# Two operand buffers of a two-block transformer kernel, laid out with a start that steps by 64 bytes every four chunks

## What is computed

```python
    z = rmsnorm(h, norm2_w) @ mlp_w1
    h = h + jnp.square(jax.nn.relu(z)) @ mlp_w2
    ...
    proj = x @ w_in                                  # 2048 columns in, about 9.5 thousand out
    merged = g_a * (o_a @ w_o_dsa) + g_b * (o_b @ w_o_moba)
    return merged @ w_out
    ...
    g, u = jnp.split(x @ w_in, 2, axis=-1)
    return (jax.nn.silu(g) * u) @ w_out
```

## The kernel before

| operand | role | residue before |
|---|---|---|
| `x_even` (the residual's normed rows, in `xa`) | moving: wide mlp up and feed-forward in, and three-matmul projections of the second block; stationary: `mv` | 144 |
| `x_held` (in `xa`) | stationary: the second block's output projection | 240 |
| `xh` (mlp's inner rows, in the region) | stationary: mlp down | 240 |
| `xk` (memory rows) | moving in the first 30 us | 240 |
| `xa` with 272 or 258 columns | moving: high part 144, low part 0 | 144 and 0 |
| `xa` from column 16 on (`from_tokens`) | moving: high part 208, low part 64 | 208 and 64 |
| `xd` with 258 columns | moving: high part 224, low part 0 | 224 and 0 |

## Time and profile before

### The profile page before, as it was taken

How to read it: one execution, slowest core, us unless ns; L and a number is a source line. 1 busy time by engine, 2 the same in 40 slices (tenths; PEclk the granted TensorE clock), 3 DMA queues, 4 the chain that set the end, 5 groups by cost and what they waited for, 6 DMA issues and landing times.

```text
span 2573.8 us, 41371 instructions
## 1 busy us (share of the span) xinstructions
PE 2555.9 (99%) x15948; PEld 2297.6 (89%) x15948; DVE 1572.9 (61%) x2178; ACT 1189.7 (46%) x1609; POOL 27.9 (1%) x70
## 2 busy tenths in 40 slices
PE   9999999999999999999999999999999999999998
PEld 7999988888888888899999999988999888888886
DVE  5444856556556555565565566666876776656665
ACT  5543545434444344544444454444544445445442
POOL 1000000000000000000000000000000000000000
PEclk9999999999999999999999999999999999999999
DMA  7664556666555665574455565565576577567753
GB/s 251 179 180 130 165 181 180 196 196 186 190 184 191 196 195 186 173 224 154 131 165 170 160 200 183 186 213 161 150 205 180 189 196 191 189 186 186 195 196 114
DMA packets 467782, 468.80 MB, mean 182 GB/s; under 512 B 9246, under 2 KB 384142, under 8 KB 466862
## 3 DMA queue, kind: packets, MB, share of 16 engines
q1 hardware_dynamic: 465600, 459.31, 58.5%
q0 software_dynamic: 2064, 7.82, 0.9%
HBM read 464.93 MB, written 2.10 MB: 181 GB/s over the span
## 4 chain that ended last, share of the span: by engine, by line
PE 97%; DVE 1%; ACT 1%; DMA 0%; issue 0%; SPq 0%; DVEq 0%; ACTq 0%
PE ps L693 17%; PE ps L696 11%; PE ps L697 11%; PE ps L698 11%; PE ps L725 11%; PE ps L727 11%; PE ps L726 11%; PE ps L694 9%; PE ps L789 1%; DMA region<-in_mem 0%; PE ps L1130 0%; PE ps L1101 0%; DVE w_lo L2091 0%; PE ps L1137 0%; PE ps L1173 0%; PE ps L1006 0%
## 5 line engine op out<-in xcount | busy, mean ns | idle before, releaser
L2091 DVE TENSOR_TENSOR w_lo<-raw,w_hi 128x1024 fp32r<-128x1024 f32 (+1 forms) x867 | 1047.5, 1219 | 766.0 <-ACT w_hi L1438 764.5
L1438 ACT ACTIVATE w_hi<-raw 128x1024 fp32r<-128x1024 f32 (+1 forms) x869 | 902.1, 1051 | 909.4 <-PE ps L727 410.1
L693 PE MATMUL ps<-xa,w_hi 128*128 128x512 f32 x1920 | 666.0, 391 | 0.0
L696 PE MATMUL ps<-xa,w_hi 128*128 128x256 f32 (+2 forms) x2112 | 607.4, 288 | 0.0
L698 PE MATMUL ps<-xa,w_lo 128*128 128x256 f32 (+2 forms) x2112 | 595.0, 282 | 0.0
L697 PE MATMUL ps<-xa,w_hi 128*128 128x256 f32 (+2 forms) x2112 | 593.4, 281 | 0.0
L694 PE MATMUL ps<-xa,w_lo 128*128 128x256 f32 x1920 | 537.3, 280 | 0.0
L693 PEld LDWEIGHTS ps<-xa,w_hi 128*128 128x128 f32 x1920 | 360.1, 188 | 79.6
L697 PEld LDWEIGHTS ps<-xa,w_hi 128*128 128x128 f32 x2112 | 398.4, 189 | 2.0 <-issue 1.0
L696 PEld LDWEIGHTS ps<-xa,w_hi 128*128 128x128 f32 x2112 | 397.2, 188 | 3.2 <-issue 2.0
L698 PEld LDWEIGHTS ps<-xa,w_lo 128*128 128x128 f32 x2112 | 396.5, 188 | 0.0
(11 more groups left out here) (364 smaller groups left out, 2537.0 us busy)
## 6 DMA issues: line engine op xcount, KB each, us to landing
raw<-in_mlp_w SPq DMA_DIRECT2D x128, 1024.0 KB
raw<-in_w_in SPq DMA_DIRECT2D x106, 1024.0 KB
raw<-in_w_ffn_in SPq DMA_DIRECT2D x176, 512.0 KB
raw<-in_w_ffn_out SPq DMA_DIRECT2D x44, 1024.0 KB
raw<-in_w_out SPq DMA_DIRECT2D x32, 1024.0 KB
raw<-in_w_o_dsa SPq DMA_DIRECT2D x8, 1024.0 KB
raw<-in_w_o_moba SPq DMA_DIRECT2D x8, 1024.0 KB
raw<-in_w_kv_mem SPq DMA_DIRECT2D x7, 1024.0 KB
```

The costliest lines, as they stand in the source:

```text
L693: nc.tensor.matmul(o, hi, x.rearrange("p a n -> p (a n)"), start=opens and ci == 0, stop=False)
L696: nc.tensor.matmul(o, hi, x_hi, start=opens and ci == 0, stop=False)
L1438: return nc.scalar.activation(dst, src, ACT.Copy, **kw)
L2091: V.tensor_tensor(w_lo[:, ps_ % CUT, 0:n], raw[:, bs % RAW, n * half:n * half + n], w_hi[:, ps_ % CUT, 0:n].bitcast(F32), ALU.subtract).th ...
```

## The change

The 16 chunks of `x_even` and the 16 of `xh` are each cut into four groups of four. Within a group the chunks stay 2048 bytes apart; each group begins `FOUR` = 2064 numbers (8256 bytes, which is 32 x 256 + 64) behind the one before. `x_even` loses its offset `EVEN` (its groups begin at residues 0, 64, 128 and 192), and `xh` loses its offset `EDGE` (its buffer begins at 224, so that its groups begin at 224, 32, 96 and 160). A group of four chunks is what one piece of weights meets in `pair`, and in `group` two pieces of two chunks. The low part of a chunk has the residue of its high part, as before. `xk`, `xm`, `xf`, `xd`, `x_held`, and `xa` with 272 or 258 columns stay as they are.

No compute instruction, DMA or wait is added, taken away or moved on any engine; six register operations of VectorE go, since the index of a group of `xh` is now the loop's own counter. What differs is the address in the operands.

```diff
+FOUR = 4 * 2 * SEQ + 16
...
-        x_even = x_rows[:, EVEN:EVEN + DC * 2 * SEQ].rearrange("p (c a n) -> p c a n", c=DC, a=2)
+        x_even = x_rows[:, 0:4 * FOUR].rearrange("p (g n) -> p g n", g=4)[:, :, 0:4 * 2 * SEQ].rearrange("p g (c a n) -> p g c a n", c=4, a=2)
+
+        def even(c):
+            return x_even[:, c // 4, c % 4]
...
-        xh = even_rows("xh", DC)
+        xh = over("xh", [P, 4 * FOUR]).rearrange("p (g n) -> p g n", g=4)[:, :, 0:4 * 2 * SEQ].rearrange("p g (c a n) -> p g c a n", c=4, a=2)
+
+        def hidden_rows(c):
+            return xh[:, c // 4, c % 4]
...
             def from_even(c):
-                return x_even[:, c]
+                return even(c)
...
-                    group(f.b0 + 16 + 4 * q, g * 32 + i * 8, f.t0 + 16 + 2 * q, g * 6 + i, held(xh),
+                    group(f.b0 + 16 + 4 * q, g * 32 + i * 8, f.t0 + 16 + 2 * q, g * 6 + i, lambda c, tb: (hidden_rows(c)[:, 0, P * tb:P * tb + P], hidden_rows(c)[:, 1, P * tb:P * tb + P]),
...
-                group(ph["mv"].b0 + 4 * g, 0, ph["mv"].t0 + 2 * g, 0, held(x_even))
+                group(ph["mv"].b0 + 4 * g, 0, ph["mv"].t0 + 2 * g, 0, lambda c, tb: (even(c)[:, 0, P * tb:P * tb + P], even(c)[:, 1, P * tb:P * tb + P]))
...
-                        copy(xh[:, bass.ds(i * 4 + (t + u), 1), 0, 0:SEQ], ut[:, u:u + 1, :]).then_inc(xb_hi, 1)
+                        copy(xh[:, bass.ds(i, 1), t + u, 0], ut[:, u:u + 1, :]).then_inc(xb_hi, 1)
...
-                        c = bass.ds(i * 4 + (t + u), 1)
-                        V.tensor_tensor(xh[:, c, 1, 0:SEQ], ut[:, u:u + 1, :], xh[:, c, 0, 0:SEQ].bitcast(F32), ALU.subtract).then_inc(xb_lo, 1)
+                        g4 = bass.ds(i, 1)
+                        V.tensor_tensor(xh[:, g4, t + u, 1], ut[:, u:u + 1, :], xh[:, g4, t + u, 0].bitcast(F32), ALU.subtract).then_inc(xb_lo, 1)
```

More of the change, by code:

```diff
@@ L359, in program @@
         TURN_W = {"n2T": V_N2, "nfT": V_FIN, "l0T": V_LG, "l1T": V_LG + 16}
-        TURN_TO = {"n2T": x_even, "nfT": x_even, "l0T": xd, "l1T": xa}
+        TURN_TO = {"n2T": even, "nfT": even, "l0T": lambda c: xd[:, c], "l1T": lambda c: xa[:, c]}
         def step_bank(key):
@@ L1512, in turned_high @@
                     w = TURN_W[name] + c
-                    ins = copy(TURN_TO[name][:, c, 0, 0:SEQ], step_bank(key)[:, i * SEQ:(i + 1) * SEQ], scale=vec[:, w:w + 1])
+                    ins = copy(TURN_TO[name](c)[:, 0, 0:SEQ], step_bank(key)[:, i * SEQ:(i + 1) * SEQ], scale=vec[:, w:w + 1])
                 ins.then_inc(turned_hi, 1)
@@ L2029, in renorm_high @@
                         act.wait_ge(re_line, c + 1)
-                        nc.scalar.activation(x_even[:, c, 0], rt[:, c % 2], ACT.Identity, bias=vec[:, V_LB + 16 + c:V_LB + 17 + c]).then_inc(re_hi, 1)
+                        nc.scalar.activation(even(c)[:, 0], rt[:, c % 2], ACT.Identity, bias=vec[:, V_LB + 16 + c:V_LB + 17 + c]).then_inc(re_hi, 1)
             side[0] = renorm_high()
@@ L2132, in turned_low @@
                     w = TURN_W[name] + c
-                    to = TURN_TO[name]
-                    ins = V.scalar_tensor_tensor(out=to[:, c, 1, 0:SEQ], in0=step_bank(key)[:, i * SEQ:(i + 1) * SEQ], scalar=vec[:, w:w + 1],
-                                                 in1=to[:, c, 0, 0:SEQ].bitcast(F32), op0=ALU.mult, op1=ALU.subtract)
+                    to = TURN_TO[name](c)
+                    ins = V.scalar_tensor_tensor(out=to[:, 1, 0:SEQ], in0=step_bank(key)[:, i * SEQ:(i + 1) * SEQ], scalar=vec[:, w:w + 1],
+                                                 in1=to[:, 0, 0:SEQ].bitcast(F32), op0=ALU.mult, op1=ALU.subtract)
                 taken(ins, key)
@@ L2903, in low @@
                     dve.wait_ge(re_hi, c + 1)
-                    V.scalar_tensor_tensor(out=x_even[:, c, 1], in0=rt[:, c % 2], scalar=vec[:, V_LB + 16 + c:V_LB + 17 + c],
-                                           in1=x_even[:, c, 0].bitcast(F32), op0=ALU.add, op1=ALU.subtract).then_inc(re_lo, 1)
+                    V.scalar_tensor_tensor(out=even(c)[:, 1], in0=rt[:, c % 2], scalar=vec[:, V_LB + 16 + c:V_LB + 17 + c],
+                                           in1=even(c)[:, 0].bitcast(F32), op0=ALU.add, op1=ALU.subtract).then_inc(re_lo, 1)
                 dve.wait_ge(piece_done, 2 * (f.b0 + 32))
```

## The result

The changed kernel takes 2590.26 us, the median of 3 runs (2590.14 to 2591.96), against 2574.75 before: a ratio of 1.0062 with a 95% interval of 1.0048 to 1.0076. It is slower by 15.5 us. The forecast was 2583 in a range of 2562 to 2602, with 0.50 on slower.

A forecast was written before the change was run, and what follows sets the result against it. The prediction took the intervals between TensorE's matmuls to bound the kernel. Terms of +3.8, -0.5 and +5.5 us gave +8.8, added with 0.95 to the 2573.8 us span for 2583.5, said as 2583, range 2562 to 2602.

The forecast's parts named there:

- What bounds the kernel: Whole kernel: time is the number of TensorE's matmuls times the interval between them; TensorE busy 2555.9 of 2573.8 us.
- The writers' term: ScalarE and VectorE writing rows at other addresses: hidden in their idle time, so nothing.
- The 0.95 us: Median of the runs above the profiled span of 2573.8 us, added to reach the forecast time.
- Term 1: `xh` as stationary operand, 1536 matmuls leaving residue 240: mean 2.45 ns, +3.8 us, bounds 0 and +7.5.
- The sign that the prediction named for itself: Mlp down stretches at some 230 to 231 ns instead of 228.3, groups of chunks 0.8 to 4 ns apart.
- Term 2: `x_even` as stationary operand in `mv`, 192 matmuls leaving residue 144: -0.5 us, bounds -0.9 and 0.
- Term 3: `x_even` as moving operand, 7056 wide and three-matmul-form matmuls: 0.78 ns each, +5.5 us, bounds -7.1 and +15.5.
- The sum: All terms over the whole kernel: +3.8 - 0.5 + 5.5 = +8.8 us.
- Rival "nothing happens": Residues average out or differences are rhythms, no property of an address: 2574.75 us, 2570 to 2580 around it; chance 0.25.
- Rival "residue 0 is cheap": Moving and stationary operands both at 0 run in step, gaining 5 ns: 2569 us, or 2543 for all residues; chance 0.25.
- Room below: TensorE's intervals: skill gives columns plus 2.5 ns, rows show 10 to 20 ns, so matmuls could also get faster.
- The rule that TensorE's two read ports don't wait on anyone: Skill's rule on moving operand and weights: by it the change does nothing and time stays 2574.75 us.

The follow-up runs named there:

- hid_only: The changed kernel's half for `xh` alone, with `x_even` kept at residue 144 as in the kernel before: 2583.76 us, ratio 1.0036 to the kernel before.
- flat0: The changed kernel without steps between groups, all `x_even` chunks at residue 0 and all `xh` chunks at 224: 2598.24 us, ratio 1.0090 to the kernel before.
- w64: The changed kernel with every group 32 bytes further on and both weight buffers at 64 instead of 0 mod 256: 2588.41 us, ratio 1.0054 to the kernel before.

## Why the prediction was right in its sign, and by half in its size

- *What bounds the kernel*: right. Nearly all of the time is in the intervals of TensorE's matmuls; ScalarE's and VectorE's idle time grew with them and ended no later. The writers' term, nothing, was right too. The 0.95 us by which a run was taken to be longer than its span is 1.7 in the later runs (2590.14 against 2588.4): the profiled execution before was one of the longer lot, with the fall of the clock in it.
- *Term 1, `xh`*: sign right, +3.8 forecast, +8.0 measured (hid_only has it alone). The step that failed is the way from 240 round to 144 by distance. The map is no slope: 240, 0, 192 and 176 are cheap, and all four of the new residues lie on the plateau around 233, so the term was at its upper bound (+7.5) and a little above. The sign that the prediction named for itself, groups 0.8 to 4 ns apart, did not show: they are at 233.2 to 233.9.
- *Term 2, `mv`*: -0.5 forecast, -0.4 measured.
- *Term 3*: +5.5 forecast, +9.5 measured. The choice to let a wide matmul shift like one of the other form was wrong: +10.3 in the wide form and -0.8 in the other. The wide form's own map has 144 as one of its best places, and 0, 64, 128, 192 cost 2.0 to 3.3 ns more a matmul than its 173.3. By the prediction's 0.78 ns the wide matmuls were worth +3.0 us and the others +2.5; the first part was more than three times too small, and the second has the wrong sign (192, put at 12.2 above the columns, has 8.8). That term 3 came out with the right sign is partly luck: the rows that it was worked out from are of the form that got faster.
- *The sum*: +17.1 in the changed stages by the trace, less 2.5 where nothing was changed, against +8.8. The range, 40 us wide, held it.
- *Rival "nothing happens"*: its cause is half true. An address can have two rhythms (flat0), but the map repeats across kernels, and w64 moved it as a whole.
- *Rival "residue 0 is cheap"*: false for a moving operand, 119.4 and 175.8, both above what 144 has (flat0's first wide stage, 173.3, is the one exception). As a stationary one in mlp down 0 is the cheapest of all, for which no row of before spoke.
- *Room below*: the lowest intervals of a stage are 113.4 ns for 256 columns and 226.8 for 512, 6.7 and 13.5 above the columns; no layout came nearer.
- *The rule that TensorE's two read ports don't wait on anyone*: by the Trainium skill (SBUF — State Buffer, section "Who interferes with whom") the time would have stayed. The runs have 113.4 to 120.0 ns for 256 columns and 226.8 to 234 for 512 by the distance of the two operands alone. The rule stands as to other engines, of which nothing was seen. As to TensorE's two operands, the time that it gives is refuted; that one port waits for the other is not shown by it. All residues here are multiples of 16 bytes, and no finer step was tried.

That it is reads of the same part of SBUF by the two streams that collide is argued, not shown: the runs show that the distance modulo 256, the lengths and the rhythm already running set the interval, and no other engine or DMA. Why two rhythms can exist at one distance, and why 258 columns come to one mean by two ways, stays open.

## What to carry to other kernels

In a kernel that is all matmuls, read the interval from start to start, and set it against columns at the granted clock; what is left (7 to 21 ns here) is partly yours. Try the start of the streaming operand against that of the stationary one, modulo 256 in steps of 16 bytes, for each shape of matmul by itself, and give each use of a buffer its own offset. Four kernels with four residues each made the whole map; a value between two measured ones could not be had by interpolation. A map made with steps is a first guide only: measure the chosen start once more in the layout that will be used, in every stage (115.5 ns became 113.4 here, and 175.8 became 176.8).

## What the runs showed that was not expected

- The distance of TensorE's two operands in SBUF, modulo 256, moves the interval of a 512-column matmul between 226.8 and 234.1 ns and of a 256-column one between 113.4 and 120.0.
- A rhythm of matmuls can be locked in for a whole stage: 173.3 and 176.8 ns a matmul from the same addresses in flat0.
- A stretch of 1462 intervals repeats to 0.01 us in 172.19, in kernels that differ elsewhere.
- After one and the same idle stretch of TensorE, 1.83 us, the granted clock falls to 1.2 GHz for 3.4 us in seven traces and stays at 2.4 in five, which is worth 1.2 to 1.5 us.
